# Folding the final norm into the first feed-forward stage, interleaving the gate stages, and starting the MLP-1 tables ahead of its norm

## The reference, cut to what matters

```python
def rmsnorm(x, g):
    y = x * lax.rsqrt(jnp.mean(x * x, axis=-1, keepdims=True) + 1e-6)
    return y * g
# first_block, layer i (0: short convolution, 1: dilated attention)
    h = h + mixed
    h = h + squared_relu_mlp(rmsnorm(h, norm_mlp[i]), mlp_w_up[i], mlp_w_down[i])
    ple_gate = jax.nn.sigmoid(rmsnorm(h, norm_ple[i]) @ ple_w_gate[i])
    h = h + ple_gate * (p[i] @ ple_w_proj[i])
return rmsnorm(h, norm_final)
# second_block starts with
    h = h + 0.5 * _swiglu(_rmsnorm(h, ffn1_norm[0]), ffn1_w_in[0], ffn1_w_out[0])
    # then an S5 state-space mixer, which needs matrices built from its parameters ("tables")
```

## Time and profile before

| | before |
|---|---|
| runs | 2053.33, 2052.52, 2049.00 us; median 2052.52 us |
| the profiled execution | 2047.45 us, of which the span from first to last instruction is 2045.6 us |
| PE busy | 1923.3 us (94% of the span) |
| DVE, ACT, POOL busy | 1303.5, 941.0, 620.1 us |
| mean granted TensorE clock | 0.978 of full speed |

### The profile page before, as it was taken

One profiled execution on the slowest core, in us unless ns is written; L12 is line 12 of the kernel. 1 busy time (PEld: TensorE's weight loads), 2 busy tenths in 40 slices (PEclk: granted clock), 3 DMA queues, 4 the chain that ended last, 5 costly groups with the idle time before them and its releaser, 6 DMA issues.

```text
span 2045.6 us, 31774 instructions
## 1 busy us (share of the span) xinstructions
PE 1923.3 (94%) x13379; PEld 1740.0 (85%) x13407; DVE 1303.5 (64%) x1509; ACT 941.0 (46%) x1228; POOL 620.1 (30%) x756
## 2 busy tenths in 40 slices
PE   8999997999988999789999899999999988889999
PEld 7989997999987999768997789999799975568998
DVE  6887666665555776556666666667566665536665
ACT  4354444444344544344444154445544454545443
POOL 6968851642332987610001600000000001320000
PEclk9999999999999999899999899999999997999999
DMA  6456663544442555446454235554255531005553
GB/s 235 181 183 222 222 230 113 185 150 145 153 156 86 203 217 211 161 155 266 185 186 180 109 126 207 217 216 164 92 200 197 197 124 42 1 1 185 186 185 103
DMA packets 54826, 336.35 MB, mean 164 GB/s; under 512 B 7915, under 2 KB 13084, under 8 KB 17820
## 3 DMA queue, kind: packets, MB, share of 16 engines
q1 hardware_dynamic: 45648, 297.51, 40.1%
q10 hardware_dynamic: 5068, 22.13, 2.8%
q0 software_dynamic: 3968, 14.68, 2.0%
HBM read 318.54 MB, written 15.75 MB: 163 GB/s over the span
## 4 chain that ended last, share of the span: by engine, by line
PE 68%; DVE 12%; POOL 9%; ACT 7%; issue 3%; DMA 1%; ACTq 0%; POOLq 0%; DVEq 0%
PE psum L468 19%; PE psum L421 10%; PE psum L423 10%; PE psum L422 10%; PE psum L470 10%; DVE w_lo L1735 4%; ACT w_hi L1013 3%; DVE both L1742 2%; POOL pw L1603 1%; POOL pw L1602 1%; POOL st L1604 1%; ACT both L1013 1%; PE psum L993 1%; PE psum L837 1%; DVE h L1748 1%
## 5 line engine op out<-in xcount | busy, mean ns | idle before, releaser
L1735 DVE TENSOR_TENSOR w_lo<-raw,w_hi 128x2048 fp32r<-128x2048 f32 x277 | 650.1, 2350 | 248.2 <-ACT w_hi L1013 245.3
L468 PE MATMUL psum<-both,w_hi 128*128 128x512 f32 x2112 | 752.4, 400 | 8.3 <-DVE both L1742 4.6
L1013 ACT ACTIVATE w_hi<-raw 128x2048 fp32r<-128x2048 f32 x280 | 533.2, 1907 | 161.1 <-PE psum L423 161.0
L470 PE MATMUL psum<-both,w_lo 128*128 128x256 f32 x2112 | 594.4, 281 | 0.0
L468 PEld LDWEIGHTS psum<-both,w_hi 128*128 128x128 f32 x2112 | 398.2, 189 | 105.9 <-DVE both L1742 6.4
L421 PE MATMUL psum<-both,w_hi 128*128 128x256 f32 x1472 | 428.5, 291 | 19.9 <-DVE both L1742 8.5
L422 PE MATMUL psum<-both,w_hi 128*128 128x256 f32 x1472 | 419.8, 285 | 0.0
L423 PE MATMUL psum<-both,w_lo 128*128 128x256 f32 x1472 | 419.7, 285 | 0.0
L470 PEld LDWEIGHTS psum<-both,w_lo 128*128 128x128 f32 x2112 | 400.5, 190 | 0.1
L421 PEld LDWEIGHTS psum<-both,w_hi 128*128 128x128 f32 x1472 | 285.1, 194 | 17.5 <-DVE both L1742 9.8
L422 PEld LDWEIGHTS psum<-both,w_hi 128*128 128x128 f32 x1472 | 285.2, 194 | 1.7 <-issue 1.2
(11 more groups left out here) (347 smaller groups left out, 2568.3 us busy)
## 6 DMA issues: line engine op xcount, KB each, us to landing
raw<-in_weights SPq DMA_DIRECT2D x280, 1024.0 KB, 4.8
table<-tables ACTq DMA_DIRECT2D x8, 1792.0 KB, 8.3
tables<-st POOLq DMA_DIRECT2D x16, 512.0 KB, 4.7
tables<-st POOLq DMA_DIRECT2D x8, 384.0 KB, 4.1
tables<-st POOLq DMA_DIRECT2D x8, 256.0 KB, 6.7
w<-in_cmp_w ACTq DMA_DIRECT2D x4, 512.0 KB, 5.1
tbl<-in_cmp_w ACTq DMA_DIRECT2D x4, 512.0 KB, 5.2
tbl<-bias_v SPq DMA_DIRECT2D x128, 16.0 KB, 5.1
```

The source lines that it names most:

```text
L468: nc.tensor.matmul(bank, wh[:, cols], both[x][:, c].rearrange("p e t -> p (e t)"), start=c == 0, stop=False, skip_group_check=True)
L470: return nc.tensor.matmul(bank[:, 0:SEQ], wl[:, cols], x_hi[x][:, c], start=False, stop=c == KC - 1, skip_group_check=True)
L1013: copy = lambda out, in_, **kw: nc.scalar.activation(out, in_, ACT.Copy, **kw)
L1735: tt(w_lo[:, g % RING], raw[:, g % RING], w_hi[:, g % RING].bitcast(F32), ALU.subtract).then_inc(sem["lo_ready"], 1)
```

## The change

**1. The final norm is folded into ffn0.** The input of ffn0 is made from the unnormed h, with the product of both gains (`fin_gain`). Both factors per token follow from two weighted sums of squares of h, one with weight 1 and one with the squared final gain (`fin_w`), which PE takes straight from the squares (`fin_sums`), without POOL's additions. h itself is multiplied by its final norm later, one chunk in each of the first eight rounds of ffn0. All 50 `keep_warm` matmuls of this place go.

**2. The gate stages are interleaved**, in both layers. ACT does the split that a gate unit frees right after the sigmoid, ahead of the residual; DVE does `x_low` of the pair before between `ta` and `tc`, and the split after each of m = 0 to 2.

**3. The first half of table 4** (the first of MLP 1) is built ahead of `norm(R_WO)`, and POOL starts it when the last attention head is written (`o_lo`) and not when the output projection is multiplied.

```diff
@@ tensor
+            def fin_sums(m):
+                pe.wait_ge(sem["fin_ready"], 1)
+                pe.wait_ge(sem["sq_ready"], PAIRS * R_FIN + m + 1)
+                if m == 0:
+                    nc.tensor.matmul(DB[3][:, 0:2 * TT], zero[:, 0:P], zero[:, 0:2 * TT], start=True, stop=False, ...)
+                for q in range(2):
+                    c = 2 * m + q
+                    for t in range(TT):
+                        last = nc.tensor.matmul(DB[3][:, 2 * t:2 * t + 2], sq[:, m % 2, q, t * P:(t + 1) * P],
+                                                fin_w[:, c], start=False, stop=c == KC - 1, skip_group_check=True)
+                last.then_inc(sem["sq_used" if m < PAIRS - 1 else "sum_ready"], 1)
...
-            keep_warm(28, U[0])
-            norm_sum(R_PLE1)
-            keep_warm(10, U[0])
-            norm_bcast(R_PLE1)
-            keep_warm(12, U[0])
             ffn(0, R_FIN)
@@ scalar, ple
                     nc.scalar.activation(tb[:], ta[:], ACT.Sigmoid).then_inc(sem["gate_ready"], 1)
-                    residual(r, m, x)
-                    if m < 2:
+                    if m < PAIRS - 1:
                         split(g + 1 + m)
-                for m in range(2, PAIRS):
-                    split(g + 1 + m)
+                    residual(r, m)
+                split(g + PAIRS)
@@ gpsimd
-            def make_table(c):
+            def make_table(c, early=None):
...
                 for n in range(1, SL + 1):
                     power(qx[:, :, :, n], qx[:, :, :, n - 1], ALU.add, ALU.subtract)
+                if early is not None:
+                    norm(early)
...
             def four_tables(c, r):
-                if c:
-                    norm(r)
-                make_table(c)
+                make_table(c, r if c else None)
...
-            pool.wait_ge(sem["unit_done"], BASE["wo"] + PAIRS)
+            pool.wait_ge(sem["o_lo"], HEADS)
             four_tables(4, R_WO)
             norm(R_MLP1)
-            norm(R_PLE1)
             norm(R_FIN)
@@ vector
+            def fin_norm():
+                dve.wait_ge(sem["sum_ready"], R_FIN + 1)
+                sums = DB[3][:, 0:2 * TT].rearrange("p (t w) -> p w t", w=2)
+                ts(fin_var[:, 0], sums[:, 0], 1.0 / D, EPS, ALU.mult, ALU.add)
+                ts(fin_m2[:], sums[:, 1], 1.0 / D, None, ALU.mult).then_inc(sem["fin_mean"], 1)
+                dve.wait_ge(sem["fin_mean"], 1)
+                stt(fin_var[:, 1], fin_var[:, 0], EPS, fin_m2[:], ALU.mult, ALU.add).then_inc(sem["var_ready"], 1)
+                dve.wait_ge(sem["rst_ready"], R_FIN + 1)
+                eye = ident.unsqueeze(1).broadcast_to([P, TT, P])
+                tt(diag[:], eye, fin_rs[:, 1].unsqueeze(2).broadcast_to([P, TT, P]), ALU.mult)
+                tt(ssum[:, 0].rearrange("p (t q) -> p t q", t=TT), eye, fin_rs[:, 0]..., ALU.mult).then_inc(sem["diag_ready"], 1)
...
@@ vector, ffn
+                    if f == 0 and k < KC:
+                        if k == 0:
+                            dve.wait_ge(sem["fin_scale"], 1)
+                        scaled = stt(h[:, k], h[:, k], col("final", k), ssum[:, 1], ALU.mult, ALU.mult)
@@ vector, ple
-                    gated(PAIRS * l + m + 1, two([XB, DB[0], DB[1], DB[2]][m]), m)
-                    if x:
-                        x_low(r, m)
-                    if m < 2:
+                    if m:
+                        x_low(r, m - 1)
+                    gated(PAIRS * l + m + 1, two([XB, DB[0], DB[1], DB[2]][m]), m)
+                    if m < PAIRS - 1:
                         split(g + 1 + m)
                     if l == 0:
                         angles(m)
-                for m in range(2, PAIRS):
-                    split(g + 1 + m)
+                x_low(r, PAIRS - 1)
+                split(g + PAIRS)
@@ vector, after mlp(1)
-            norm(R_PLE1)
-            dve.wait_ge(sem["rs_ready"], R_PLE1 + 1)
-            for m in range(PAIRS + 1):
-                if m < PAIRS:
-                    for q in range(2):
-                        c = 2 * m + q
-                        last = stt(h[:, c], h[:, c], col("final", c), rs[:, 0], ALU.mult, ALU.mult)
-                    last.then_inc(sem["h_ready"], 1)
-                if m:
-                    x_low(R_FIN, m - 1)
```

More of the change, by code:

```diff
@@ L354, in hbase, with gain @@
         def hbase(r):
-            return PAIRS * (r - 1)
+            return PAIRS * (r - 1 + (r > R_FIN))
+        def gain(r, c):
+            return fin_gain[:, c:c + 1] if r == R_FIN else col(GAIN[r], c)
         def chunk(ap, c, n=1):
@@ L434, in _ @@
             PB = [XB, DB[0], DB[1], DB[2]]
-            GB = [DB[3], U[0], U[1], DB[3]]
+            GB = [[DB[3], U[0], U[1], last] for last in (DB[3], MB)]
             def up_unit(g0, k, x, bank, arrive=None, mid=None):
@@ L1030, in x_high @@
                     c = 2 * m + q
-                    last = copy(x_hi[XBUF[r]][:, c], h[:, c], scale=col(GAIN[r], c))
+                    last = copy(x_hi[XBUF[r]][:, c], h[:, c], scale=gain(r, c))
                 last.then_inc(sem["xh_ready"], 1)
@@ L1049, in norm @@
                 last.then_inc(sem["rs_ready"], 1)
+                if n == R_FIN:
+                    copy(ssum[:, 1], norm_bank(n)[:, 0:SEQ]).then_inc(sem["fin_scale"], 1)
             def residual_stage(stage, r):
```

80 lines of the change are left out of this document (62 added, 18 removed).

## The result

The changed kernel takes 1997.25 us (median of 4 runs, 1997.12 to 1997.61), the kernel before beside it 2051.89 us (4 runs): ratio 0.9746, 95% interval 0.9732 to 0.9761.

What follows compares the result with a forecast made beforehand. TensorE, busy 94% of a 2045.6 us span, was taken as the bound. Terms 13.5 + 7.0 + 16.5 = 37 us, less 1 for missed lateness, gave 36 off 2052.52: 2016 us, 8 in 10 from 2008 to 2028.

Steps and rivals of the forecast that it cites:

- the 1.0 us lost ahead of MLP 1: Norm ahead of MLP 1: the early half table ends late and delays it by 1.0 us, bounds 0 and 8.6.
- 11.5 + 3.0: MLP 1: TensorE's wait on the fourth table goes, 11.5 us, and the half clock behind it, 3.0 us.
- A margin that I called safe: MLP 1: fourth `tab_ready` near 806, TensorE wants it at 822.5, so 16 us to spare, 8 at the bound.
- move along: MLP 1 tables: store transfers and the place in the ring shift with the tables, all later ones some 29 us early.
- the cycle of 6.3 us: Gate stage 0: ACT and DVE take 6.3 us per gate, with 0.6 to 0.9 us for angle instructions.
- angles stretched: Part of the rival that gate stages gain less, 4 and 12 us for 7 and 16.5: 2024 us, chance 0.11.
- The 1.1 us taken off: Gate stage 1 into ffn0: 17.6 us cut to 16.5 for an extra copy, table loads on ACT and half clock.
- the 15.9 us: Gate stage 1 into ffn0: the gain if idle gaps without warming matmuls bring half clock; 17.6 without a drop.
- Three places count: Whole kernel: gains come only from MLP 1's table wait, gate stage 0, and gate stage 1 into ffn0; 37 us in sum.
- more than forecast: Rival: all bounds at their good end, 40.5 us, and no clock drop ahead of gate stage 1: 2010 us, chance 0.06.
- slower: Rival: ffn0 without warming matmuls stays at half clock, costing 85 us over its 170: 2102 us, chance 0.03.
- I carry the difference over to the median unchanged: Whole kernel: the profiled execution, 2047.45 us, lies 5.1 us below the median, 2052.52; this gap was assumed to stay.

Runs made afterwards that it cites:

- tables_only: Kernel before with only the early half table and its wait on the last head, no tensor moved: 2036.38 us, ratio 0.9925.
- pad192: Kernel before with only 192 unused bytes per partition added behind nhalf, shifting the tensors behind: 2036.08 us, ratio 0.9933.
- gates0_only: Kernel before with the interleaved order in gate stage 0 alone, nothing moved in memory: 2045.63 us, ratio 0.9965.
- fold_gates1: Changed kernel with the old gate stage 0 order and old place of the tables; folded norm, gate stage 1 and 192 bytes stay: 2023.6 us, ratio 0.9855.
- no_warm: Kernel before without its 50 matmuls on zeros around the final norm: 2051.88 us, ratio 1.0003.
- after_back: Changed kernel with 64 more unused bytes behind its small tensors, so those behind lie 256 bytes further than before: 2008.87 us, ratio 0.9799.
- the two benches: Separate kernels without the computation, only matmuls from tiles at known addresses; 256-column matmuls took 283 ns at distance 0 and 276 at 192 in the first.
- the second bench: Separate kernel without the computation: 512+256-column pairs and threes of 256 at eight distances from the weights; pairs 354 ns at 0, 348 at 32.

## Why the prediction was wrong

**Edit 3, the tables: right.** 13.5 us forecast; 13.4 in the stage, 14.5 (*tables_only*) in the whole. The half table takes 20.9 us for 22.4; the 1.0 us lost ahead of MLP 1 did not occur, as POOL's first addition (640.69) is 7.9 us earlier than in the earlier trace rows and so is the norm behind it. In its place stands the wait of 1.3 us on `w_lo` in the list of waits, for the second unit of MLP 1, which *tables_only* and, without this edit, *pad192* have too and before has not. So 11.5 + 3.0 less 1.3 us come near the forecast, but the loss is another one than forecast. The fourth `tab_ready` came at 809.60 + 0.50 = 810.1, which with the stage 7.9 us early is 818 by the time of before, not 806, and PE turned that table at 813.9: 3.8 us to spare and not 16. A margin that I called safe was thin: the four `tab_ready` are 29, 29, 20 and 16 us earlier than before by the time of before. That store transfers "move along" was wrong in part, as POOL's waits for the tables' stores grew from 13.1 to 16.1 us in this stretch. The clock is 1.00 there.

**Edit 2 in gate stage 0: right mechanism, gain put too high.** 7.0 forecast, 5.1 measured (6.8 +- 3.5 by *gates0_only*). The term that was off is the cycle of 6.3 us: 6.1 once, then 7.1 and 7.4. It had the angle instructions at 0.6 to 0.9 us a gate in all; POOL's additions stretch one of them by 1.1 us each time. I had taken this as part of a rival (angles stretched) and not into the sum. The wait of 4.5 us (4.9) and the half clock behind it were as forecast.

**Edits 1 and 2 from gate stage 1 into ffn0: right mechanism, gain put too low.** 16.5 forecast, with a bound of 18; 18.7 in the trace, 18.3 in *fold_gates1*. The cycle is 5.4 for 5.6 us, TensorE waits 0.2 and 1.5 us where 0.6 and 1.8 were worked out, and no half clock follows. The 1.1 us taken off, for this among other things, were not needed. Nor did the 15.9 us come that the prediction gives by the Trainium skill (TensorE: Matmul & The Clock Gate, section Why this matters for your kernels). By it idle gaps between bursts bring the half clock; the trace agrees behind 4.91 and 2.3 us of waiting and shows no drop behind 1.50. *no_warm* shows the other side, a drop that cost nothing measurable. The scaling of h in ffn0 was hidden, as said.

**Sum of the edited places:** 37 forecast, 37.2 measured. That the two agree so closely is luck: one part came out 1.9 us below and another 2.2 above. What failed stands outside them.

**The step that failed** is "Three places count": the change was read from its instructions alone, and the sum 13.5 + 7.0 + 16.5 has no term for the rest of the kernel. The five tensors move all that is allocated behind them by 192 bytes, and I priced the allocation at nothing without looking at it. It is worth 10.3 us in the matmuls of five stages (MLP 0, MLP 1, ffn0, ffn1 and ffn3), which no edit touches. *pad192* (13.7 by its ratio, 10.5 to 17.0, with 4.6 of the S5 mixer in it) and *after_back* (11.6 lost again) show the cause. No rival held it; "more than forecast" ended at 2010 and had only good ends of my own terms. The rival "slower" also rests on a wrong reading: "the longest such stretch here ends 6 us after the work resumes" does not hold in the trace of before, where the clock is 0.50 for the 8 us from 1132.5 and low for some 3 us more (the S5 mixer above).

**Two smaller ones.** First, "I carry the difference over to the median unchanged": the profiled execution before lay 4.4 us under the median of its runs, that of after on it, and the changed kernel's runs lie within 0.5 us of each other. That is 4.4 us of the 54.6. Second, the S5 mixer, 4.6 us less with less half clock in it, at which nothing in the edits aims. Together: 37.2 + 10.3 + 4.6 - 1.8 in the other stages = 50.3 of span, and 4.3 to 4.4 for the median. The longer sparse attention stage (199.9 for 197.9 us, 201.5 in *after_back* and *fold_gates1*, but 196.1 in *pad192*) belongs to those 1.8 and was not traced to its cause.

## What to carry to other kernels

Compare the allocations of two kernels as well as their instructions: a tensor added in the middle moves all behind it, a gain in unedited stages points there, and one kernel with nothing but the padding settles it. Where that may be in a comparison, time the change in two placements; here the edits alone are worth 42 us and look like 55. And a wait on another engine eats what is gained upstream of it: with faster matmuls alone MLP 1 stayed at 215 us, and only with the tables early did it drop by another 2.

## What was not expected of the hardware

- Matmuls of 256 f32 columns, each with its weight load, were spaced 119.6 to 120.0 ns when the moving operand lies 0 bytes past the weights by the remainder of 256, 117.9 at 64, and 113.6 or 117.9 at 192; 6 ns on 120 is 5%. In the two benches it is the distance of the two addresses and not the address of either, and in the first traffic of ACT, DVE and DMA did not change it. Pairs with 512 columns show another pattern in the second bench: 354 ns at 0 and at 192, 348 at 32.
- At 192, and now and then at 64, a stretch keeps one of two paces to its end. What picks it is open.
- After the same wait of 4.2 us on the same instruction the granted clock was 0.50 for 4 us of work in one kernel and 11 us in another.
